# Scan levels in the projection, the first loads split over two queues, and q/k items ahead of gate and value items

## Chip, cores and metric

The kernel runs on one core of one Trainium2 chip, written in Bass: every engine has its own instruction stream, and streams wait for each other by semaphores. The metric is device time in microseconds. A profiled execution gives a span from its first to its last recorded instruction; the time that counts for it is a little longer.

## What is computed

Two layers of a backbone over 640 tokens: one tile of 128 context tokens and four tiles of latent tokens, width 1024, all in float32. A layer is

```python
h = rms_norm(x, norm1_g) * (1.0 + sc1) + sh1
qa, ia, fza, fzb, ga, qg, kg, vg, qw, kw, vw = split_proj(h @ w_in)      # 1024 -> 2560
o_a, s_a = hgrn_mixer(qa, ia, fza, fzb, ga, lb, a_norm_g, s_ctx)         # gated scans, both ways
o_g = blocked_attention(rope_2d(qg), ...)                                # all latent + cached keys
o_w = banded_attention(rope_2d(qw), rope_2d(kw), vw, ck_w, cv_w, sink)   # |t-s| <= 128
x = x + g1 * (jnp.concatenate([o_a, o_g, o_w], axis=-1) @ w_out)
h = rms_norm(x, norm2_g) * (1.0 + sc2) + sh2
x = x + g2 * moe(h, router_w, router_b, w_gate_up, w_down)               # top 2 of 16 experts
```

The shifts, scales and gates (sh1 to g2) are `silu(cond) @ mod_w + mod_b`, 6144 columns in twelve blocks of 512. A scan is `S = d * S + k v`, `o = q S`, for four heads, forward and backward, with a decay per channel.

## The kernel before

Each layer is a row of program sections (`nc.Block()`). At the end of a section all engines wait for each other. The sections that matter here:

**Setup** (lines 245 to 320): SyncE (SP) issues the loads of constants, masks and small vectors, then x (lines 267 to 269), four blocks of `mod_w` (line 271) and the layer's parameters (`load_params`, lines 240 to 243). SP's queue takes transfers in order, and an issue is held up while the queue is full.

**Norm 1** (lines 416 to 495): ScalarE squares x (line 465) and scales it (line 469). TensorE transposes it (lines 434 and 439), and in layer 0 it also computes the first four mod blocks (`cond_rows`, line 367; `turn_rows`, line 374). ScalarE and VectorE write the modulated `hT` (lines 476, 491, 494). SP loads `w_in` in five blocks; two of them wait until the transposes have read `xn`, which lies in their place.

**Projection** (lines 513 to 700): SP loads the cached keys and values (lines 516 to 519), TensorE transposes the keys (lines 533, 534), then come six items with turned output (four of gates, two of q and i, lines 544 and 545), five value items `ia` (line 571), ten q/k items `glob` and `win`, tile by tile (lines 577 and 580), and five `rest` items (line 574). An item is eight k-steps. Of a q/k item ScalarE copies the result (line 619), VectorE squares, sums and normalises it with a power from GpSimd (line 628) and rotates it (lines 691 to 696), TensorE transposes it (line 555), VectorE copies that into `qT` and `kT` (lines 652, 653).

**Attention** (lines 717 to 1240): 30 units (tile, head group, global or windowed); a loop of 32 steps does scores (line 911) of one unit, products with values (line 937) of the one before last, and transposes (line 923) of the last. VectorE finds the maxima (lines 1118, 1123), ScalarE takes the exponentials (line 1033), both copy turned probabilities (lines 1148, 1055), and VectorE writes the outputs of a pair of units (line 1159). Beside them run 81 **side steps**, three to a loop step, each waiting until the one before has been read (`s_free`):

- the scan's intra-tile scores by doubling: 8 levels x 5 tiles, four products each (level 0 on line 957, levels 1 to 7 on line 962, rows of 64). VectorE merges each result under a mask into `Am` (line 1173). After a level GpSimd multiplies keys and queries by the decays of the level's half blocks (lines 882, 887) and makes the next block products (line 874), and ScalarE merges the keys of both directions (line 1062). A level waits for both.
- after each level the next mod block: rows (line 367), ScalarE copy (line 1076), turn (line 374), VectorE add (line 1179).
- then ten pairs of keys (line 976) and state (line 980), and five outputs (lines 990, 995).

Behind the loop VectorE normalises the scan's output (lines 1230 to 1236), with a power from GpSimd (line 892), and the output projection follows (gate rows line 1249, `w_out` products line 1287). `sides_before` says which side steps a loop step has:

```python
            SIDE_START = 0
            THIRDS = 3
...
                return min(NSIDE, max(0, THIRDS * (step - SIDE_START) + part))
```

## Time and profile before

| | us |
|---|---|
| median of 3 runs | 1786.13 |
| lowest, highest | 1782.95, 1787.25 |
| the profiled execution | 1782.59 |
| its span | 1780.7 |
| TensorE busy in it | 1426.5 (80%) |
| VectorE, ScalarE, GpSimd busy | 567.3, 370.9, 198.7 |
| granted clock of TensorE, mean | 0.889 |

Stages of layer 0 by the stage table and the timeline: setup to 31.9, norm 1 to 63.8, projection from 79.2 to 260.8, attention to 501.8, output projection to 584, then norm 2, routing and experts; layer 1 begins its norm near 920. A busy TensorE is not one at its peak, and idle time of an engine that nobody waits for costs nothing.

### The profile page before, as it was taken

How to read it: one execution, taken by the hardware profiler on the slowest of the kernel's cores; microseconds unless marked ns; L12 is line 12 of the kernel's file. 1: busy time of each engine (PE TensorE's matmuls, PEld its weight loads, DVE VectorE, ACT ScalarE, POOL GpSimd, SP SyncE). 2: the span in 40 equal slices, each digit the busy share in tenths (PEclk: the TensorE clock that was granted, in tenths of full speed). 3: DMA queues.
4: the chain of work that ended last, by engine and by line, in shares of the span. 5: the costliest groups of instructions: out<-in, count | busy, mean ns of one | idle time of the engine just before them, and what ended most of it. 6: DMA issues, size and time to landing. Idle time of an engine off the chain costs nothing. (4 is left out here: it accounts for less than half of the span.)

```text
span 1780.7 us, 18938 instructions
## 1 busy us (share of the span) xinstructions
PE 1426.5 (80%) x6940; PEld 912.6 (51%) x6941; DVE 567.3 (32%) x1145; ACT 370.9 (21%) x745; POOL 198.7 (11%) x171
## 2 busy tenths in 40 slices
PE   0699998898879859999308999889886984999950
PEld 0357745677744724444105775557775454444420
DVE  0111524555421531111042053346443144111115
ACT  3111012334410301111031100233342021111113
POOL 0000113421010000000010010242201000000001
PEclk9799995999989869999758999789998995999985
DMA  9500014317010578999620000432200004799933
GB/s 330 189 1 3 1 42 153 121 70 275 1 47 0 209 271 290 369 369 352 233 84 7 0 4 3 145 134 105 98 1 0 0 30 165 255 368 365 359 114 142
DMA packets 111945, 254.12 MB, mean 143 GB/s; under 512 B 9832, under 2 KB 18432, under 8 KB 111872
## 3 DMA queue, kind: packets, MB, share of 16 engines
q1 hardware_dynamic: 93712, 199.64, 31.6%
q0 software_dynamic: 8064, 29.36, 4.5%
q10 hardware_dynamic: 10096, 24.12, 3.5%
q8 instruction: 49, 0.80, 0.2%
q14 instruction: 24, 0.20, 0.0%
HBM read 221.91 MB, written 34.34 MB: 144 GB/s over the span
## 5 line engine op out<-in xcount | busy, mean ns | idle before, releaser
L1670 PE MATMUL PS<-W,T 128*128 128x512 f32 x544 | 242.6, 599 | 4.5 <-ACT T L1712 4.5
L1670 PEld LDWEIGHTS PS<-W,T 128*128 128x128 f32 x544 | 104.3, 192 | 135.9 <-issue 130.1
L1287 PE MATMUL PS<-W,T 128*128 128x512 f32 x320 | 138.9, 593 | 2.3 <-ACT T L1300 2.3
L577 PE MATMUL PS<-W,hT 128*128 128x384 f32 x320 | 129.8, 487 | 0.0
L1688 PE MATMUL PS<-W,T 128*128 128x512 f32 x272 | 126.0, 607 | 1.4 <-ACT T L1736 1.4
L937 PE MATMUL PS<-T 128*128 128x64 f32 x864 | 112.1, 283 | 3.2 <-ACT T L1055 1.9
L937 PEld LDWEIGHTS PS<-T 128*128 128x128 f32 x864 | 105.1, 198 | 15.6 <-issue 8.5
L544 PE MATMUL PS<-hT,W 128*128 128x512 f32 x192 | 102.1, 615 | 0.0
L1287 PEld LDWEIGHTS PS<-W,T 128*128 128x128 f32 x320 | 60.2, 190 | 75.5 <-issue 72.7
L1761 DVE TENSOR_TENSOR T<-PS,T 128x256 f32<-128x256 f32 x34 | 14.5, 426 | 243.7 <-ACT T L1723 243.7
L911 PE MATMUL PS<-T 64*128 64x128 f32 (+3 forms) x480 | 70.0, 407 | 18.0 <-ACT T L1055 13.4
L580 PEld LDWEIGHTS PS<-W,hT 128*128 128x128 f32 x320 | 60.8, 190 | 42.3
L1628 POOL DMA_INDIRECT T<-h_rows,T x36 | 34.0, 946 | 428.8 <-PE PS L1660 323.2
L1757 DVE COPY T<-PS 128x1024 f32<-128x1024 f32 x34 | 41.7, 1226 | 119.4 <-PE PS L1688 119.4
L1173 DVE COPY_PREDICATED hT<-levelmask,PS 128x512 f32<-128x512 uint8 x80 | 59.1, 739 | 60.7 <-PE PS L962 47.1
L1723 ACT ACTIVATE T<-PS 128x256 f32<-128x256 f32 x34 | 13.1, 386 | 311.6 <-PE PS L1670 311.6
L962 PE MATMUL PS<-W 64*128 64x128 f32 x560 | 62.0, 348 | 19.6 <-ACT W L1062 10.7
L1688 PEld LDWEIGHTS PS<-W,T 128*128 128x128 f32 x272 | 50.1, 194 | 52.8 <-issue 52.8
L1033 ACT ACTIVATE T<-PS,small 128x640 f32<-128x640 f32 (+1 forms) x72 | 46.2, 647 | 119.7 <-DVE small L1137 94.7
L911 PEld LDWEIGHTS PS<-T 64*128 64x128 f32 x480 | 50.4, 207 | 39.4 <-DVE T L1148 21.4
L574 PE MATMUL PS<-W,hT 128*128 128x512 f32 x160 | 69.7, 592 | 0.0
L923 PE MATMUL PS<-cst,T 128*128 128x128 f32 x432 | 66.7, 301 | 0.0
(272 smaller groups left out, 1960.0 us busy)
## 6 DMA issues: line engine op xcount, KB each, us to landing
W<-in_w_gate_up SPq DMA_DIRECT2D x34, 2048.0 KB, 12.5
W<-in_mod_w SPq DMA_DIRECT2D x20, 2048.0 KB, 8.2
W<-in_w_down SPq DMA_DIRECT2D x34, 1024.0 KB, 10.6
y_rows<-T ACTq DMA_DIRECT2D x34, 512.0 KB, 8.8
W<-in_w_in SPq DMA_DIRECT2D x6, 2048.0 KB, 17.1
T<-in_mod_w SPq DMA_DIRECT2D x4, 2048.0 KB, 19.4
W<-in_w_out SPq DMA_DIRECT2D x2, 4096.0 KB, 13.8
y_rows<-cst SPq DMA_DIRECT2D x1, 7680.0 KB, 32.9
```

The costliest lines, as they stand in the source:

```text
L544: pe.matmul(PS[:, i % 2, :], lhsT, hT[:, k, P:TOK], start=(k == 0), stop=(k == KC - 1))
L574: last = pe.matmul(out, lhsT, wblk[:, B_REST, k, :], start=(k == 0), stop=(k == KC - 1))
L577: pe.matmul(out[:, 0:QW].rearrange("p (j v d) -> p j v d", v=KVH, j=G), lhsT, w[:, 0:QW].rearrange("p (v j d) -> p j v d", v=KVH, j=G), st ...
L580: last = pe.matmul(out[:, QW:512], lhsT, w[:, QW:512], start=False, stop=(k == KC - 1), skip_group_check=True)
L911: last = pe.matmul(PS[:, bank, at * P:(at + m) * P], qT[kv_rows, wnd, j, col(t)], kT[kv_rows, wnd, kt * P:(kt + m) * P], start=True, stop= ...
L923: last = pe.transpose(PS[:, bank, col(at)], pr[wnd][:, col(kv * len(keys) + n)], ident)
L937: last = pe.matmul(PS[:, 5, at:at + HD], src[:, col(kv * len(keys) + n)], v[:, kt, kv * HD:(kv + 1) * HD], start=(n == 0), stop=(n == len( ...
L962: last = pe.matmul(out, KM[rows_r, f, col(t)], both_ways(QD[rows_r].rearrange("p d f n -> p d (f n)"), at_t, P, h), start=True, stop=True)
L1173: dve.copy_predicated(Am[:, t, :, :], levelmask[:, lv:lv + 1, :].to_broadcast([P, AH, P]), PS[:, 6:8, 0:2 * P]).then_inc(s_free, 1)
L1287: last = pe.matmul(PS[:, 4 + 2 * (t % 2) + b, :], oT[:, t % 2, k, :], wout[:, k, col(b, 512)], start=(k == 0), stop=(k == KC - 1))
L1670: last = pe.matmul(PS[:, 2 + par, :], hgT[:, par, k, :], w[:, k, :], start=(k == 0), stop=(k == KC - 1))
L1688: last = pe.matmul(PS[:, 6 + b, :], haT[:, par, col(f)], w[:, f, col(b, 512)], start=(f == 0), stop=(f == 1))
```

## The change

- **Loads.** x is loaded from ScalarE's queue. The cache loads of layer 0 go into the setup, those of layer 1 into norm 1. Of the four first mod blocks two are issued in the setup, two in norm 1, with the q/i block of `w_in` behind them; the other four blocks of `w_in` are issued in the projection's section. The blocks' places in SBUF change, so that none waits for `xn`.
- **Order of the projection.** The q/i items and the value items come first, then the four gate items, then the q/k items of all tiles, then the rest (gate and value) items. The results go round three PSUM banks instead of four; transposes have one bank instead of two.
- **Levels.** The 8 levels x 5 tiles go out of attention into the k-loop of the last 15 items: a slot after every second k-step, five slots of products, then two without. They have two pairs of PSUM banks in turn. The level's products on GpSimd, the key merges on ScalarE and the masked copies on VectorE go with them. The work of VectorE on a q/k item is cut into four pieces, one per slot, and the squares of the norm go to ScalarE.
- **Attention.** 41 side steps are left, two to a loop step: keys, state, mod rows, mod turn, in turn. The scan's closing normalisation goes into the loop, one of its four parts in each of the steps 25 to 28.

```diff
+            sp.dma_start(ck[:, 0, :], cgk[0, l].rearrange("s h d -> s (h d)")).then_inc(s_cl, 16)
+            sp.dma_start(ck[:, 1, :], cwk[0, l].rearrange("s h d -> s (h d)")).then_inc(s_cl, 16)
+            sp.dma_start(vg[:, NT, :], cgv[0, l].rearrange("s h d -> s (h d)")).then_inc(s_cl, 16)
+            sp.dma_start(vw[:, NT, :], cwv[0, l].rearrange("s h d -> s (h d)")).then_inc(s_cl, 16)
...
-                sp.dma_start(x[:, 0, :], x_prompt[0]).then_inc(s_x[0], 16)
-                for t in range(1, NT):
-                    sp.dma_start(x[:, t, :], x_sample[0, (t - 1) * P:t * P, :]).then_inc(s_x[t], 16)
-                for n in range(MOD1):
-                    sp.dma_start(modw[:, n, :, :], mod_w[0, :, col(n, 512)].rearrange("(k p) n -> p k n", p=P))\
-                      .then_inc(s_mh[n], 16)
+                load_cache(sp, 0)
+                for n in range(2):
+                    load_first_mod(sp, n)
                 load_params(sp, 0)
...
             def _(act):
+                act.dma_start(x[:, 0, :], x_prompt[0]).then_inc(s_x[0], 16)
+                for t in range(1, NT):
+                    act.dma_start(x[:, t, :], x_sample[0, (t - 1) * P:t * P, :]).then_inc(s_x[t], 16)
...
                 def _(sp):
                     if layer == 0:
-                        for b in (B_GATES, B_QI, B_GLOB):
-                            load_win(sp, b, 0)
-                        sp.wait_ge(s_tr, 1 + KC)
-                        for b in (B_WIN, B_REST):
-                            load_win(sp, b, 0)
+                        for n in range(2, MOD1):
+                            load_first_mod(sp, n)
+                        load_win(sp, B_QI, 0)
+                    else:
+                        load_cache(sp, layer)
...
+            late = [(kind, t) for t in range(NT) for kind in ("glob", "win")] + [("rest", t) for t in range(NT)]
+            qk_late = [n for n, it in enumerate(late) if it[0] != "rest"]
+            NQ = len(qk_late)
+            REST0 = late.index(("rest", 0))
+            ITEM0 = NT
+            NLEV = len(LEVELS) + 1
+            SLOTS, FIRST_SLOT, GAP = 4, 3, 2
...
+            def level_in(q):
+                i = q - FIRST_SLOT
+                if i < 0 or i >= NLEV * (NT + GAP) or i % (NT + GAP) >= NT:
+                    return None
+                return i // (NT + GAP), i % (NT + GAP)
...
+            def merge_in(q):
+                i = q - FIRST_SLOT
+                if i < 0 or i % (NT + GAP) != NT + GAP - 1:
+                    return None
+                lv = i // (NT + GAP) + 1
+                return lv if lv < NLEV else None
...
+            def turn_after(n):
+                return qk_late.index(n - 2) if n - 2 in qk_late else None
...
+                    if layer == 0:
+                        for b in (B_GATES, B_GLOB, B_WIN, B_REST):
+                            load_win(sp, b, 0)
...
+                    def columns_turned(b, c0, parity):
                         for k in range(KC):
                             lhsT = wblk[:, b, k, col(c0)]
...
+                    pe.wait_ge(s_win[B_GATES], 16)
+                    for i in range(4):
...
                     def turn(m):
                         pe.wait_ge(s_rot, m + 1)
...
+                        for c in range(4):
+                            last = pe.transpose(PS[:, 3, col(c)], rr[:, m % 2, c, :], ident)
+                        last.then_inc(s_tp, 1)
+                    def level(lv, t):
+                        i = lv * NT + t
+                        if i == 0:
                             pe.wait_ge(s_cte, 1)
...
+                            pe.wait_ge(s_gr, 1)
+                            pe.wait_ge(s_qm, 2)
+                        if i >= 2:
+                            pe.wait_ge(s_lc, i - 1)
+                        if t == 0 and lv >= 1:
+                            pe.wait_ge(s_hm, lv)
+                            pe.wait_ge(s_km, lv)
+                        for a in range(AH):
+                            f, r = a // 2, a % 2
+                            rows_r = slice(64 * r, 64 * r + 64)
+                            out = PS[:, 4 + 2 * (i % 2) + r, col(f)]
+                            if lv == 0:
+                                for d in range(2):
+                                    last = pe.matmul(out, KK[rows_r, d, f, col(t)], QQ[rows_r, f, col(t)],
+                                                     start=(d == 0), stop=(d == 1))
+                                continue
+                            last = pe.matmul(out, KM[rows_r, f, col(t)],
+                                             both_ways(QD[rows_r].rearrange("p d f n -> p d (f n)"), f * TOK + t * P, P,
+                                                       LEVELS[lv - 1]), start=True, stop=True)
+                        last.then_inc(s_lp, 1)
...
+                    for n, (kind, t) in enumerate(late):
...
+                            if k == KC - 1:
+                                last.then_inc(s_z, 1)
+                            if k == 3 and turn_after(n) is not None:
+                                turn(turn_after(n))
+                            if k % 2:
+                                step = level_in(SLOTS * n + k // 2)
+                                if step is not None:
+                                    level(*step)
...
+                    pool.memset(Am, 0.0).then_inc(s_am0, 1)
+                    pool.wait_ge(s_gr, 1)
...
+                    for d in range(2):
+                        last = pool.tensor_tensor(qd[:, 1 - d, :], qq, fgate[:, d, :], ALU.mult)
+                    last.then_inc(s_hm, 1)
...
+                        flow(last)
+                    def update(lv):
+                        h = LEVELS[lv - 1]
+                        nb = 2 * TOK // (2 * h)
+                        product = fgate if h == 1 else BP[h]
+                        pool.wait_ge(s_lp, NT * (lv + 1))
+                        pool.wait_ge(s_hm, lv)
+                        for d in range(2):
+                            ks, qs = (0, 1) if d == 0 else (1, 0)
+                            of_q = pairs(product, d)[:, :, qs:qs + 1].to_broadcast([P, nb, h])
+                            last = pool.tensor_tensor(halves(kd, d, h, ks), halves(kd, d, h, ks), of_q, ALU.mult)
+                        last.then_inc(s_hk, 1)
+                        for d in range(2):
+                            ks, qs = (0, 1) if d == 0 else (1, 0)
+                            of_k = pairs(product, d)[:, :, ks:ks + 1].to_broadcast([P, nb, h])
+                            last = pool.tensor_tensor(halves(qd, 1 - d, h, qs), halves(qd, 1 - d, h, qs), of_k, ALU.mult)
+                        last.then_inc(s_hm, 1)
...
+                    block_products(fgate, BP[2])
+                    for q in range(SLOTS * len(late)):
+                        n = q // SLOTS - 1
+                        if q % SLOTS == 0 and n in qk_late and late[n][0] == "glob":
+                            pool.wait_ge(s_rd, late[n][1] + 1)
+                            pool.tensor_tensor(small[:, 88:96], small[:, 96:104], minus_half[:, 0:8],
+                                               ALU.pow).then_inc(s_rp, 1)
+                        step = level_in(q)
+                        if step is not None and step[0] >= 1 and step[1] == NT - 1:
+                            lv = step[0]
+                            update(lv)
+                            if lv < NLEV - 1:
+                                block_products(BP[2 * LEVELS[lv - 1]], BP[4 * LEVELS[lv - 1]])
...
+                    def level_copy(lv, t):
+                        i = lv * NT + t
+                        dve.wait_ge(s_lp, i + 1)
+                        if i == 0:
+                            dve.wait_ge(s_am0, 1)
+                        b = 4 + 2 * (i % 2)
+                        dve.copy_predicated(Am[:, t, :, :], levelmask[:, lv:lv + 1, :].to_broadcast([P, AH, P]),
+                                            PS[:, b:b + 2, 0:2 * P]).then_inc(s_lc, 1)
...
+                    def piece(m, s):
+                        t, w = m // 2, m % 2
+                        if s == 0:
+                            dve.wait_ge(s_ze, ITEM0 + qk_late[m] + 1)
+                        if w == 0:
+                            if s == 0:
+                                means(m)
+                            elif s == 1:
+                                normed(m)
+                            elif t > 0:
+                                rotated(m, s - 2)
+                            return
+                        if s == 0 and m >= 2:
+                            dve.wait_ge(s_tp, m - 1)
+                        if t == 0:
+                            if s == 0:
+                                dve.tensor_copy(rr[:, 1, :, :], zr[:, 1, :, :]).then_inc(s_rot, 1)
+                        elif s < 2:
+                            if t == 1 and s == 0:
+                                dve.wait_ge(s_co, 2 * 16)
+                            rotated(m, s)
+                    dve.wait_ge(s_par, 4 * 16 * (layer + 1))
+                    for n in range(len(late)):
+                        for s in range(SLOTS):
+                            if n - 1 in qk_late:
+                                piece(qk_late.index(n - 1), s)
+                            if s == 2 and turn_after(n) is not None:
+                                turned_evac(turn_after(n))
+                            step = level_in(SLOTS * n + s)
+                            if step is not None:
+                                level_copy(*step)
+                    for m in left_over:
...
-            for lv in range(NLEV):
-                side_steps += [("level", lv, t) for t in range(NT)]
-                side_steps += [("mod_rows", MOD1 + lv), ("mod_turn", MOD1 + lv)]
-            assert MOD1 + NLEV == 12
             for n in range(len(STATE_STEPS)):
                 side_steps += [("keys", n), ("state", n)]
+                if n < 12 - MOD1:
+                    side_steps += [("mod_rows", MOD1 + n), ("mod_turn", MOD1 + n)]
...
+            PER_STEP = 2
+            RMS_STEP = 25
...
-                return min(NSIDE, max(0, THIRDS * (step - SIDE_START) + part))
+                return min(NSIDE, max(0, PER_STEP * (step - SIDE_START) + min(part, PER_STEP)))
...
                     for step in range(U + 2):
+                        if RMS_STEP <= step < RMS_STEP + 4:
+                            scan_norm(step - RMS_STEP)
```

## Rows read from the trace of the kernel before

**Rows 1.** Stage table: stretch, length, busy PE, PEld, DVE, ACT, POOL, clock, DMA share, GB/s.
```profile
64.00:79.20 15.20, 0.00 (x0) 0.00 (x0) 0.00 (x0) 0.39 (x1) 0.00 (x0) 0.50 0.96 293
79.20:260.80 181.60, 180.55 (x714) 113.41 (x714) 48.19 (x115) 20.46 (x54) 8.19 (x6) 0.98 0.01 2
260.80:501.80 241.00, 197.49 (x1560) 158.32 (x1560) 123.38 (x270) 81.70 (x199) 59.90 (x47) 0.86 0.34 122
```
**Rows 2.** Timeline of the start: start, duration, engine, line, operation, wait.
```profile
7.87 16.39 SPq L271 DMA_DIRECT2D T<-in_mod_w  x4
...
24.30 5.29 SPq L240 DMA_DIRECT2D qkg<-in_q_norm_g  x1
...
31.97 1.06 ACT L465 ACTIVATE W<-x 128x1024 f32<-128x1024 f32 x1 [19.14 <-PEq L245]
...
63.09 0.72 DVE L494 TENSOR_SCALAR hT<-PS,scale,modc 128x128 f32<-128x128 f32 x2
...
71.98 2.42 SPq L516 DMA_DIRECT2D small<-in_cache_glob_k  x1
```
**Rows 3.** Stage table while the first loads run.
```profile
24.00:28.00 4.00, 0.00 (x0) 0.00 (x0) 0.00 (x0) 0.00 (x0) 0.00 (x0) 1.00 1.05 387
```
**Rows 4.** Timeline of TensorE, first instruction of layer 1's projection.
```profile
944.30 0.48 PE L533 MATMUL PS<-cst,small 128*128 128x128 f32 x1 [5.22 <-DMA T<-in_cache_win_v]
```
**Rows 5.** Timeline of TensorE in attention: a level unit and its follower.
```profile
343.32 0.72 PE L962 MATMUL PS<-W 64*128 64x128 f32 x8
343.96 2.44 PE L937 MATMUL PS<-T 128*128 128x64 f32 x20
```
**Rows 6.** Timeline of ScalarE in the projection: evacuation of a q/k item.
```profile
165.53 0.60 ACT L619 ACTIVATE T<-PS 128x512 f32<-128x512 f32 x1 [6.35 <-PE PS L580]
```
**Rows 7.** Attention's groups (busy, mean ns, idle before and why), then GpSimd's timeline.
```profile
L962 PE MATMUL PS<-W 64*128 64x128 f32 x280 | 31.2, 350 | 9.7 <-ACT W L1062 5.3 <-DVE hT L1173 2.5 <-POOL W L887 1.6
...
L1173 DVE COPY_PREDICATED hT<-levelmask,PS 128x512 f32<-128x512 uint8 x40 | 29.6, 739 | 30.1 <-PE PS L962 23.7 <-PE PS L957 6.3
...
L882 POOL TENSOR_TENSOR T<-T,hT 128x640 f32<-128x640 f32 x12 | 16.0, 1357 | 72.3 <-PE PS L962 72.3
...
L957 PE MATMUL PS<-T 64*128 64x128 f32 x80 | 9.4, 389 | 5.0 <-DVE hT L1173 5.0
...
293.53 3.62 POOL L882 TENSOR_TENSOR T<-T 128x640 f32<-128x640 f32 x2 [20.49 <-PE PS L962]
...
404.50 2.48 POOL L882 TENSOR_TENSOR T<-T,hT 128x640 f32<-128x640 f32 x2 [14.57 <-PE PS L962]
```
**Rows 8.** Timelines of GpSimd and VectorE in attention, then groups of the projection.
```profile
351.34 2.62 POOL L887 TENSOR_TENSOR W<-W,hT 128x640 f32<-128x640 f32 x2
351.44 1.25 DVE L1133 TENSOR_TENSOR small<-small,sink 128x2 f32<-128x2 f32 x1
...
L628 POOL TENSOR_TENSOR small<-small,minus_half 128x8 f32<-128x8 f32 x5 | 8.2, 1637 | 174.3 <-DVE small L669 174.3
...
L693 DVE TENSOR_TENSOR T<-T,cst 128x256 f32<-128x256 f32 x8 | 3.4, 425 | 0.3
```
**Rows 9.** Timeline of VectorE: outputs of pairs of units, and the stage's end.
```profile
431.21 0.42 DVE L1159 TENSOR_TENSOR W<-PS,small 128x256 f32<-128x256 f32 x1
...
445.25 0.42 DVE L1159 TENSOR_TENSOR W<-PS,small 128x256 f32<-128x256 f32 x1
...
462.18 0.43 DVE L1159 TENSOR_TENSOR W<-PS,small 128x256 f32<-128x256 f32 x1
...
473.82 0.42 DVE L1159 TENSOR_TENSOR W<-PS,small 128x256 f32<-128x256 f32 x1
...
483.69 0.42 DVE L1159 TENSOR_TENSOR W<-PS,small 128x256 f32<-128x256 f32 x1
...
492.88 0.42 DVE L1159 TENSOR_TENSOR W<-PS,small 128x256 f32<-128x256 f32 x1
...
499.79 1.49 DVE L1236 TENSOR_TENSOR W<-T,small 128x1280 f32<-128x1280 f32 x1 [1.97 <-POOL small L892]
```

463 lines of the change are left out of this document (204 added, 259 removed).

## Prediction

> **What bounds the kernel now.** I read the stage table first. The projection of layer 0 (79.2 to 260.8) has TensorE busy for 180.6 of 181.6 us: it is TensorE's own work, and whatever is put into it is paid for. The attention stage (260.8 to 501.8) has it busy for 197.5 of 241.0 us at a clock of 0.86 [rows 1]; layer 1 repeats both stages, and I count everything twice. So 43.5 us per layer of that stage are waits, and the change moves 40 small products from the stage with waits into the one without. Between 64.0 and 79.2 the engines do next to nothing [rows 1].
>
> Then the timeline of the start, to see what that silence is. SP hands out four blocks of mod_w (16.4 us for 4 issues, so it is held up by what is already queued), then the small parameter loads (5.3 us for the first), and only after them does its program section end; ScalarE takes up the norm at 31.97. The norm's last write ends at 63.8, the cache loads are issued at 72 because SP is still handing out w_in, and TensorE starts at 79.2 [rows 2]. In that stretch the DMA engines move 387 GB/s [rows 3]. In layer 1 the same cache loads cost TensorE 5.2 us of waiting [rows 4].
>
> **Start of layer 0.** The change takes two of the four mod_w blocks and the x loads out of SP's first section; x (2.6 MB) goes through ScalarE's queue, the cache loads go ahead of mod_w. Ahead of the parameters then stand about 1.2 MB of constants and masks, 0.3 of cache and 4.2 of mod_w, with x beside them. Before, the parameters got through when some 1.2 of the 4 blocks were still to come (issue ends 29.6; 12.3 MB in all would end near 36 at 387 GB/s) [rows 2, 3]. With the same rule and two blocks fewer (4.2 MB, 10.8 us) the section ends near 19; x used the slow first microseconds less than it could have, so I take 18 and as bounds 15 and 25. From ScalarE's first instruction to the last write of the norm it is 31.8 us [rows 2], which holds mod rows that need blocks 2 and 3; those land by about 36, before the 18 + 23 at which the last is used. Projection at 18 + 32.3 + 0.5 = 50.8, against 79.2: **28 us less** (21 to 31). The w_in block for q and i comes next in the queue, 2.1 MB or 5.4 us later (near 41), so it is there; the gate block is issued at 51 and is wanted only after 2 q/i items of 640 columns and 5 value items of 256. By 6.95 us for 8 steps of 512 columns [rows 6] these take 17.4 and 17.4 us, so near 85; the other blocks are wanted later still.
>
> **Start of layer 1.** Cache loads issued a section earlier: most of the 5.2 us go, not some 1.4 for the norm's last writes and the hand-over of sections: **3.8 us less** (3 to 4.5) [rows 4].
>
> **Projection: what is added.** Eight levels x 5 tiles = 40 units. A warm unit of levels 1 to 7 holds TensorE from 343.32 to 343.96, 0.64 us [rows 5]; one of level 0, with twice the products, twice that. 35 x 0.65 + 5 x 1.2 = 28.8 us. They now stand between the k-steps of the 512-column items, of which no row shows a price. The 0.64 was measured between foreign work too, so I add only 0.05 us a unit, 2 us in all (bounds 0 and 0.3 us a unit, 12 in all). Reordering the items adds and removes nothing: one of 512 columns goes on taking 6.95 us (6.35 of waiting and 0.60 of evacuation on ScalarE) [rows 6].
>
> Between two levels stand three slots of two k-steps, 5.13 us, or 5.6 where four transposes fall in them. In that time GpSimd must do its four products of the level: mean 1.36 us each, 1.81 at the first level and 1.24 at the last [rows 7], so about 7.3, 6.2, 5.5, 5.3, 5.1 and 5.0 us from the first to the sixth. Without anything in their way that leaves some 1.9 + 1.3 + 0.1 us of TensorE waiting, and 1.4 where a power for the norm (L628, 1.64 us [rows 8]) is ahead of them: 5 us.
>
> But something is in their way. VectorE's small operations end exactly where a GpSimd product ends: L1133, which touches 2 elements a row, took 1.25 us while L887 ran [rows 8]. The two exclude each other, one instruction at a time. In attention VectorE mostly reads PSUM; in the projection it has, per pair of items, three multiplications for the norm and twelve of 0.42 us for the rotation [rows 8], all from SBUF to SBUF. Followed instruction by instruction, with one VectorE operation let in after each product, level 2 goes so: the last product of level 1 ends 7.5 us into its item, GpSimd's four take 4 x 1.81 and three rotation operations of 0.42 come between, ready at 16.1; TensorE has three slots and four transposes (5.6) and stands there at 13.0: it waits 3.1 us. By the same steps level 3 waits 2.4, level 4 3.1 (the power stands ahead of the products), level 5 2.0 (the power stands behind them, so the norm and the copies of level 5 are late); levels 6 and 7 fall where no rotation is left, 0.1. Sum 10.7 us. VectorE's level copies (40 x 0.74 = 29.6 us [rows 7]) fit: 48.2 us of VectorE work become 78 in a stage of 220 [rows 1]. No step of the projection is moved past SP's stores.
>
> Sum: 28.8 + 2 + 10.7 = 41.5, **42 us more per layer** (34 to 54); the window becomes 181.5 + 42 = 223.5.
>
> **Attention: what goes.** In pairs of units (global and windowed of one head group) the time between outputs (L1159) is 9.87 us with no side work (473.82 to 483.69) and 14.04 with six side steps of keys and states (431.21 to 445.25) [rows 9]. New pairs have four: keys, state, mod rows, mod turn. They have less hand-over but the mod rows are longer, so I take the near row, 14.0 us, bounds 12.5 and 15.5, for pairs 3 to 7; 13.2 for pair 8 with four of keys and states (between the two); 16.9 for pair 9 with four output steps and 11.6 for pair 10 with one, as the pairs that end at 462.18 and 473.82; then 10.6 (one more key tile), 9.9, 9.9, 9.2, plus 1.5 for the closing norm, which now lies on VectorE between those units (four operations of 1.5 us, each covered by the scores of the next unit where VectorE has nothing to do). The first three pairs (context tile) cost more than their work: the very first state step now needs the state loads, which stand behind 4.2 MB of mod_w in the queue: 10.8 us at 387 GB/s [rows 3] and some 3 us around it, 14 us (before, nothing asked for them until the levels were done). VectorE waits for them with the next unit's maximum behind it, so TensorE stands too. Then 8.7 us a pair, of bare hand-overs: an estimate with no row of its own, it is 5.3 under the 14.0 of later tiles for the scores, transposes and weighing that the context tile hardly has (bounds 6 and 12). 14 + 3 x 8.7 = 40. Sum: 40 + 70 + 13.2 + 16.9 + 11.6 + 10.6 + 29 + 1.5 = 192.8, and of the tail (L1236 ended the stage at 501.3, 8 us behind the last output at 493.3 [rows 9]) 0.6 stays: 193.4, taken as 194, against 241: **47 us less per layer** (35 to 57). The check from the other side: the level products had 31.2 + 9.4 us of TensorE with 9.7 + 5.0 of waits ahead of them [rows 7], 55.3; with the tail 63; less the new 14 us wait, 49.
>
> **The sum.** 1782.6 (the profiled execution; its span is 1780.7) - 28 - 3.8 + 2 x (42 - 47) = 1740.8. The median of the runs shown is 1786.1, 3.5 more, so in medians 1786.1 - 41.8 = **1744**. The edit to the two stages nearly cancels; the loads are the gain.
>
> **Rivals.**
> 1. *GpSimd and VectorE do not collide* (the two stages overlap less often than I laid them, or attention loses more waits): projection +36, attention -50: 1786.1 - 31.8 - 28 = 1726. For it: the clash shows only on VectorE's side [rows 8], GpSimd's products were never seen to wait. Chance 0.14, for 1705 to 1728.
> 2. *Attention is paced by hand-overs, not by TensorE*: scores, maximum, exponential, copy in turn, with the side steps in line behind them. Then a step taken out gives nothing as long as others wait at the same place: pairs 3 to 7 stay at the 16.9 us of the slowest pair without levels [rows 9] instead of 14.0, 14.5 more, and the closing norm is uncovered at 6 us instead of 1.5. The stage is 213, the gain 28 for 47; 2 x 19 more: 1782. For it: 43.5 us of waits in the stage [rows 1], of which only 14.7 stand ahead of level products [rows 7]. Against: with no side work at all a pair falls to 9.87 [rows 9]. Chance 0.17, for 1766 to 1792: 0.10 faster, 0.06 no measurable change, 0.01 slower.
> 3. *Slower: VectorE wins the port.* In the rows GpSimd runs its products back to back and VectorE gets one in between. If a run of six rotation operations (2.5 us) goes ahead of each product instead, an update is 10 us longer minus the 1.8 already counted; at the four levels that meet rotations that is 32 us a layer, 64 in all: 1808. It decides from 21 us of extra waits a layer on. Against: L1133 was let in alone [rows 8]. Chance 0.07. The Trainium skill, SBUF — State Buffer, section "Who interferes with whom", calls this an exclusive lock held for a whole instruction and says that the order of issue decides who blocks; by it this rival's order is as allowed as mine, and a multiplication with both inputs in SBUF is among those that collide. The trace agrees on the whole instruction (1.25 us for 2 elements a row) and shows only one of the two orders.
>
> My forecast keeps 0.62, for 1728 to 1766. **Range**: 1715 to 1780, which leaves out the far end of rival 1, the upper part of rival 2 and rival 3, under 2 in 10. Runs of this kernel tell 0.3% (5.4 us) from no change. Faster by more: 0.62 + 0.14 + 0.10 = 0.86; within: 0.06; slower: 0.07 + 0.01 = 0.08.
>
> **What would show it.** TensorE's first projection product near 51 (right from 45 to 57); the wait for the cache gone in both layers. Projection windows of 223 us with TensorE waits in front of the level products, released by GpSimd, about 3 us at levels 2 to 4 and none at 6 and 7. VectorE multiplications of 1.3 us and more in place of 0.42 while products run. Attention windows of 194 us, 14 of them at the start behind the state loads, and no 8 us tail. It is wrong if attention stays over 205, if the projection passes 235, or if ScalarE still begins the norm after 25.

## The result, and the profile after

The changed kernel takes 1803.97 us (median of 4 runs, 1799.56 to 1806.74), the kernel before on the same chip 1784.54 (1782.29 to 1787.25). The ratio is 1.0088 with a 95% interval of 1.0052 to 1.0124: **0.9% slower**, where 1744 us and 2.3% faster were forecast. Another order of the same side steps then gave 1744.16 us, and the experiments say why. Of all executions behind the times of this document one, the fourth of run slot_early, was slow without a known reason (8134.28 us), and it is left out of that run's median.

The profiled execution of after is 1799.56 us long with a span of 1797.7, 17.0 longer than the span before. The stage table of after for layer 0, projection and attention (stretch, length, busy PE, PEld, DVE, ACT, POOL, granted clock, DMA share, GB/s):

```profile
53.20:277.20 224.00, 216.97 (x1074) 138.03 (x1073) 89.39 (x150) 32.94 (x66) 64.15 (x51) 0.99 0.12 39
277.20:495.10 217.90, 167.31 (x1201) 130.29 (x1201) 86.92 (x230) 71.24 (x192) 5.33 (x2) 0.85 0.37 134
```

Against [rows 1], the projection begins 26 us earlier, is 43 us longer and stands at a granted clock near full speed. The attention is only 23 us shorter: TensorE is busy 30 us less in it but waits 51 us for 44, at the same low mean clock. Its other products kept it busy for 163.2 us before (the trace's records without L957 and L962, merged), and the same ones do so for 167.3 now. The timelines of SP and ScalarE at the start of after answer [rows 2]:

```profile
7.70 2.78 SPq L241 DMA_DIRECT2D T<-in_mod_w  x2
10.52 6.84 SPq L254 DMA_DIRECT2D qkg<-in_q_norm_g  x1
...
20.38 0.38 SPq L241 DMA_DIRECT2D T<-in_mod_w  x1
20.40 1.06 ACT L478 ACTIVATE W<-x 128x1024 f32<-128x1024 f32 x1 [2.55 <-PEq L259]
```

The parameter loads are held up still (6.84 us for the first), yet they are through at 20 and ScalarE begins the norm at 20.40 instead of 31.97. At the start of layer 1, TensorE waits 1.35 us where [rows 4] had 5.22:

```profile
939.78 0.30 PE L576 MATMUL PS<-cst,small 128*128 128x128 f32 x1 [1.35 <-PEq L427]
```

TensorE's groups in the attention of after (line, busy, mean ns of one, idle before and what ended it):

```profile
L1061 PE MATMUL PS<-T 64*128 64x128 f32 (+2 forms) x240 | 37.6, 433 | 25.9 <-ACT T L1182 13.1 <-DVE T L1258 11.7 <-PEq L557 1.1
...
L380 PE MATMUL PS<-W,condT 128*32 128x512 f32 x128 | 21.9, 817 | 11.3 <-DVE T L1299 11.3
```

L1061 are the scores; TensorE waits 25.9 us ahead of them, for the copies of the transposed weights (L1182 on ScalarE, L1258 on VectorE). The same group in the kernel before waited 9.0:

```profile
L911 PE MATMUL PS<-T 64*128 64x128 f32 (+3 forms) x240 | 34.7, 404 | 9.0 <-ACT T L1055 6.7 <-DVE T L1148 1.1 <-PEq L513 1.1
```

One pair of steps of after shows the place (TensorE's timeline; L1073 transposes, L1061 scores, L1106 keys, L1087 weighing, L1110 state):

```profile
372.18 1.29 PE L1073 MATMUL PS<-cst,T 128*128 128x128 f32 x10
374.46 2.50 PE L1061 MATMUL PS<-T 64*128 64x384 f32 x8 [0.99 <-ACT T L1182]
376.89 0.69 PE L1106 MATMUL PS<-cst,T 128*128 128x128 f32 x2
377.37 2.58 PE L1087 MATMUL PS<-T 128*128 128x64 f32 x20
380.71 0.71 PE L1110 MATMUL PS<-T,W 128*128 128x128 f32 x4 [0.76 <-ACT W L1192]
381.26 0.82 PE L1073 MATMUL PS<-cst,T 128*128 128x128 f32 x6
383.08 1.15 PE L1061 MATMUL PS<-T 64*128 64x256 f32 x12 [1.00 <-DVE T L1258]
```

Between the transposes and the next scores stands nothing, and each time TensorE waits 1 us for the copy. Before, one side step of three stood there. (A plain product is two records of the timeline, a transpose is one: the x4 of L1110 are two products.)

**Where the time went**, from TensorE's first product of the projection, its first scores and the first product behind the attention, in us:

| stretch | before | after | difference |
|---|---|---|---|
| start to projection, layer 0 | 79.7 | 53.2 | -26.5 |
| projection, layer 0 / 1 | 181.1 / 180.4 | 224.1 / 224.1 | +43.0 / +43.7 |
| attention, layer 0 / 1 | 241.0 / 240.2 | 217.9 / 217.5 | -23.1 / -22.7 |
| behind it up to projection 1 | 443.0 | 444.9 | +1.9 |
| behind it to the end | 415.4 | 416.1 | +0.7 |

The sum is +17.0, as the spans say. The +1.9 hold the 3.9 us that layer 1's start gained and 5.8 lost behind layer 0's attention. Of the kernels below some are some 6 us shorter in that stretch and some are not, whatever was edited, and I give the 5.8 to no part of the change. The last stretch varies as well, from 413.9 to 424.6 us, in kernels that differ only ahead of it. So a part is judged by its stage's length, and the kernel's time alone does not settle less than some 10 us.

### The profile page after: what moved, and what is told of

It reads as the page before. It is cut to its first block and busy times, and to the rows that moved or that the text cites. A ratio compares the mean times of both kernels' runs of the same rounds, so it can differ in the third digit from the quotient of the medians.

```text
span 1797.7 us, 18955 instructions
## 1 busy us (share of the span) xinstructions
PE 1448.3 (81%) x6940; PEld 912.0 (51%) x6941; DVE 577.4 (32%) x1135; ACT 375.0 (21%) x755; POOL 201.5 (11%) x171
## 3 DMA queue, kind: packets, MB, share of 16 engines
q1 hardware_dynamic: 92992, 197.01, 30.8%
## 5 line engine op out<-in xcount | busy, mean ns | idle before, releaser
L657 PE MATMUL PS<-W,hT 128*128 128x384 f32 x320 | 137.5, 512 | 0.0
L1087 PEld LDWEIGHTS PS<-T 128*128 128x128 f32 x864 | 105.0, 198 | 25.5 <-issue 19.5
L1061 PE MATMUL PS<-T 64*128 64x128 f32 (+2 forms) x480 | 74.2, 429 | 50.8 <-ACT T L1182 26.1
L1087 PE MATMUL PS<-T 128*128 128x64 f32 x864 | 111.1, 282 | 3.2 <-ACT T L1182 1.9
L582 PE MATMUL PS<-hT,W 128*128 128x512 f32 x192 | 98.3, 594 | 0.0
L825 DVE COPY_PREDICATED W<-levelmask,PS 128x512 f32<-128x512 uint8 x80 | 58.2, 727 | 109.6 <-PE PS L637 87.4
L1873 DVE TENSOR_TENSOR T<-PS,T 128x256 f32<-128x256 f32 x34 | 14.5, 426 | 243.6 <-ACT T L1835 243.6
L1061 PEld LDWEIGHTS PS<-T 64*128 64x128 f32 x480 | 52.0, 216 | 74.5 <-DVE T L1258 62.6
L380 PE MATMUL PS<-W,condT 128*32 128x512 f32 x336 | 61.5, 873 | 26.5 <-DVE T L1299 21.5
L655 PE MATMUL PS<-W,hT 128*128 128x512 f32 x160 | 76.2, 610 | 0.0
L637 PE MATMUL PS<-W 64*128 64x128 f32 x560 | 52.8, 308 | 12.0 <-issue 9.8
## 6 DMA issues: line engine op xcount, KB each, us to landing
W<-in_w_gate_up SPq DMA_DIRECT2D x34, 2048.0 KB, 12.4
W<-in_w_down SPq DMA_DIRECT2D x34, 1024.0 KB, 10.6
W<-in_w_in SPq DMA_DIRECT2D x6, 2048.0 KB, 17.4
```

Of the source, the lines that this page charges most:

```text
L380: last = pe.matmul(PS[strip, bank, :], condT[:, k, :], w[:, k, :], start=(k < 4), stop=(k >= 4), skip_group_check=True)
L582: pe.matmul(PS[:, parity, :], lhsT, hT[:, k, P:TOK], start=(k == 0), stop=(k == KC - 1))
L637: last = pe.matmul(out, KM[rows_r, f, col(t)], both_ways(QD[rows_r].rearrange("p d f n -> p d (f n)"), f * TOK + t * P, P, LEVELS[lv - 1]) ...
L655: last = pe.matmul(out, lhsT, w, start=(k == 0), stop=(k == KC - 1))
L657: pe.matmul(out[:, 0:QW].rearrange("p (j v d) -> p j v d", v=KVH, j=G), lhsT, w[:, 0:QW].rearrange("p (v j d) -> p j v d", v=KVH, j=G), st ...
L825: dve.copy_predicated(Am[:, t, :, :], levelmask[:, lv:lv + 1, :].to_broadcast([P, AH, P]), PS[:, b:b + 2, 0:2 * P]).then_inc(s_lc, 1)
```

## The experiments

Two theories stood at first. By my prediction's sum, a level step costs TensorE's time wherever it stands, and the attention of after must have got something new that eats the gain. By the **cover theory**, the level steps of the old attention stood in time in which TensorE would have waited anyway, so the attention gives little back for them while the projection pays in full. The runs will show a third thing, the granted clock, beside both.

Each ratio is to the kernel before on the same chip; the chips of the runs differ. A median is of 3 to 10 executions, "one time" is a single one. Stage lengths are measured as in the table above, in one profiled execution, layer 0 / layer 1.

| run | us (median) | ratio, 95% interval | projection | attention |
|---|---|---|---|---|
| loads | 1753.56 | 0.9814, 0.9792 to 0.9837 | 180.1 / 178.6 | 240.1 / 239.6 |
| loads_norm | 1745.12 | 0.9767, 0.9746 to 0.9787 | 178.6 / 178.6 | 238.5 / 232.1 |
| early_mods | 1796.18 | 1.0047, 1.0016 to 1.0078 | 225.5 / 224.1 | 213.5 / 209.8 |
| att_empty | 1778.46 | one time | 179.8 / 180.6 | 236.7 / 237.1 |
| filler | 1826.09 | 1.0218, 1.0164 to 1.0273 | 225.6 / 224.1 | 227.0 / 230.0 |
| three | 1778.94 | 0.9946, 0.9913 to 0.9980 | 225.5 / 224.1 | 203.0 / 196.3 |
| proj_empty | 1753.78 | one time | 201.3 / 199.9 | 217.5 / 217.9 |
| proj_nopool | 1778.79 | one time | 216.2 / 216.2 | 218.0 / 220.0 |
| pairs | 1803.53 | 1.0079, 1.0039 to 1.0119 | 228.0 / 225.8 | 218.7 / 219.3 |
| all3 | 1773.85 | 0.9899, 0.9867 to 0.9930 | 228.4 / 225.8 | 194.5 / 194.4 |
| att_double | 1832.65 | one time | 181.3 / 180.5 | 265.4 / 257.6 |
| att_nopool | 1781.49 | one time | 181.3 / 180.5 | 232.2 / 227.8 |
| slot | 1744.16 | 0.9774, 0.9732 to 0.9817 | 225.6 / 224.1 | 190.6 / 188.3 |
| att_refill | 1793.59 | 1.0038, 1.0017 to 1.0058 | 181.3 / 180.6 | 245.0 / 238.0 |
| att_empty2 | 1781.19 | 0.9967, 0.9949 to 0.9986 | 181.2 / 180.6 | 234.4 / 237.1 |
| slot_early | 1731.45 | 0.9706, 0.9678 to 0.9735 | 222.4 / 224.1 | 181.1 / 179.0 |

### The loads alone, and the loads with the closing norm

Run loads is the kernel before with the change's first loads; its main lines:

```diff
-                for t in range(1, NT):
-                    sp.dma_start(x[:, t, :], x_sample[0, (t - 1) * P:t * P, :]).then_inc(s_x[t], 16)
-                for n in range(MOD1):
-                    sp.dma_start(modw[:, n, :, :], ...
+                load_cache(sp, 0)
+                for n in range(2):
+                    load_first_mod(sp, n)
```

> The kernel before with one part of the change alone: the first loads split (x through ScalarE's queue, two mod_w blocks ahead of the parameters and two behind, the cache loads of each layer one section earlier). The order of the projection and of the attention is that of before. If the parts add up as the trace of after says, the projection of layer 0 starts at 52 to 54 (before 79.2), the one of layer 1 some 4 us nearer to its norm, the rest is untouched: 1784.5 - 26.3 - 4.2 = 1754 us. Rival: the early start only helps because the q/i block comes first in the new order, and here the gates block of before arrives too late: then less than 15 us of the 26 are left, 1765 us or more.

Measured: 1753.56 us, and the projection of layer 0 starts at 55.5. The gain of the loads is what it should be, and it needs no new order of the projection's items. By difference the rest of the change costs some 49 us (1.0088 against 0.9814).

Run loads_norm adds the change's scan_norm, called in the loop (steps 27 to 30, where the change has 25 to 28) instead of behind it:

```diff
+                        if RMS_STEP <= step < RMS_STEP + 4:
+                            scan_norm(step - RMS_STEP)
```

> The kernel before with the new first loads and with the closing norm of the recurrence spread over steps 27 to 30 of the attention loop instead of behind it. The level steps stay in the attention. In the kernel before, the last output stands at 492.9 and the stage ends at 501.8; with the norm inside the loop, the stage should end near 494 to 496: 6 to 8 us less per layer, so 1754 - 14 = 1740 us, faster than before by 2.5%. If the norm's four operations of 1.5 us are not covered by the scores of the next units, half of it is left: 1747 us.

Measured: 1745.12 us, 8.4 less than loads for 14 expected. Layer 1 gained 7.5 us of its attention and layer 0 only 1.6.

### What the level work costs the projection

proj_empty and proj_nopool cut the change's level steps. In both, GpSimd's updates touch one block:

```diff
-                            of_q = pairs(product, d)[:, :, qs:qs + 1].to_broadcast([P, nb, h])
+                            of_q = pairs(product, d)[:, 0:1, qs:qs + 1].to_broadcast([P, 1, h])
```

proj_empty has, besides, one product of 2 columns per step:

```diff
-                        for a in range(AH):
+                        for a in range(1):
...
-                            out = PS[:, 4 + 2 * (i % 2) + r, col(f)]
+                            out = PS[:, 4 + 2 * (i % 2) + r, 0:2]
```

> The changed kernel with the level steps of the projection emptied in place: one product of 2 columns instead of four or eight of 128, masked copies of 2 columns, GpSimd's updates on the first block only (the recurrence's result is not computed; block products, merging of keys and the place of every step are kept). What the level work costs the projection is what goes: by my sum 28.8 of products + 2 for their insertion + 10.7 of waits = 41.5 us per layer; by the trace of after 36.7 of TensorE's time + 6 of waits. Either way the stage goes from 224 to 182 to 185 us and the kernel to about 1722 us. The rival here is that the emptied steps still cost 0.2 to 0.3 us each because they break into the stream of products: then 190 us or more, 1735 us.

> The changed kernel with GpSimd's updates in the projection cut to the first block of each level (the recurrence's result is wrong by that), while TensorE does all level products. If the price of a level step (0.90 us in the stream) is the products' own, only TensorE's waits ahead of the levels go, 6 us per layer: stage at 218, kernel at 1792 us. VectorE's multiplications of the rotation, 1.2 to 2.1 us while GpSimd works, should take 0.42 us again. If my term of 10.7 us for the collision was right and the products cost 0.72 us, the stage should lose 10 us or more: 1783 us.

The emptied projection is 201.3 us, not 182: the rival of that expectation holds, and its 0.2 to 0.3 us a step is still too little. TensorE's timeline of proj_empty:

```profile
146.50 0.38 PE L659 MATMUL PS<-W,hT 128*128 128x128 f32 x2
146.81 0.38 PE L637 MATMUL PS<-W 64*128 64x2 f32 x2
147.12 0.91 PE L656 MATMUL PS<-W,hT 128*128 128x384 f32 x2
...
149.05 0.38 PE L637 MATMUL PS<-W 64*128 64x2 f32 x2
```

From emptied step to emptied step it is 2.24 us, with two k-steps of 0.87 between them: a single product of 2 columns costs 0.50 us of the stream. In after, a full one of four products costs 2.61 - 1.74 = 0.87. The wait of 2.13 us ahead of the first row is one of four such; the others are 1.49, 1.31 and 1.06 us:

```profile
169.40 1.03 PE L637 MATMUL PS<-W 64*128 64x128 f32 x8 [2.13 <-issue]
...
173.61 0.75 PE L637 MATMUL PS<-W 64*128 64x128 f32 x8
...
176.22 0.75 PE L637 MATMUL PS<-W 64*128 64x128 f32 x8
```

Without GpSimd's updates the stage is 216.2, 7.9 us less, and TensorE is busy without a gap; 216.2 is 35.1 over the projection of before. The products cost more than these 35.1: the projection of before starts at a granted clock of 0.50 (79.2 to 84.0) and that of after at 1.00 (53.0 to 58.0), and the largest group of the first items takes 49.1 us (L582 in after) for 51.4 (L544 in before, the same 96 records). So of the 43 us some 37.5 are products, 8 are what the updates cost, and some 2.5 came back by the clock at the start.

The 8 are not all collision. TensorE's four waits sum to 6.0 us, where the prediction had 5 without a collision and 10.7 with it. VectorE's side of the collision is plain, in after (GpSimd, then VectorE):

```profile
165.29 4.01 POOL L778 TENSOR_TENSOR W<-W,T 128x640 f32<-128x640 f32 x2
165.53 2.10 DVE L860 TENSOR_TENSOR T<-T,cst 128x256 f32<-128x256 f32 x1
167.56 2.03 DVE L861 TENSOR_TENSOR T<-T,cst 128x256 f32<-128x256 f32 x1
```

The same VectorE line in proj_nopool:

```profile
163.89 0.42 DVE L860 TENSOR_TENSOR T<-T,cst 128x256 f32<-128x256 f32 x1
```

GpSimd's side is small: its four products of this level take 3.80 + 4.01 = 7.81 us (161.52 to 169.30) where the same four in the attention of before took 3.62 + 3.67 = 7.29 (293.53 to 300.78).

Run pairs does two level steps after every fourth k-step instead of one after every second:

```diff
-                            if k % 2:
-                                step = level_in(SLOTS * n + k // 2)
-                                if step is not None:
-                                    level(*step)
+                            if k % 4 == 3:
+                                for q in (SLOTS * n + k // 2 - 1, SLOTS * n + k // 2):
+                                    step = level_in(q)
+                                    if step is not None:
+                                        level(*step)
```

> The changed kernel with the level steps of the projection done two at a time: instead of one after every second k-step, two after every fourth. Products, copies and updates are the same, in the same order. In the run with emptied level steps a step of one 2-column product still cost 0.50 us of the stream (the next two k-steps started 2.24 us later instead of 1.74). If that is the price of leaving the stream of 128-row products and coming back, it is paid 20 times less per layer: 20 x 0.5 = 10 us, 1804 - 20 = 1784 us. If it is the product's own price (weights of 128 columns), nothing changes: 1804 us.

Measured: nothing gained. In the timeline of pairs, TensorE's two steps together stand from the last k-step to the next one so:

```profile
150.04 0.38 PE L660 MATMUL PS<-W,hT 128*128 128x128 f32 x2
150.35 1.59 PE L637 MATMUL PS<-W 64*128 64x128 f32 x16
151.87 0.91 PE L657 MATMUL PS<-W,hT 128*128 128x384 f32 x2
```

1.83 us from k-step to k-step instead of the bare 0.22, and the k-step behind is 0.10 longer: 1.71 for eight products, 2 x 0.87 done singly. My theory of a price for leaving the stream is wrong. Products in the stream cost 0.21 to 0.22 each when there are four or eight and 0.50 when there is one of them; what makes up the 0.50 was not tried.

### What the level work cost the attention

Four kernels edit the attention of before. att_empty empties products, masked copies and updates; att_nopool the updates alone; att_double does each product twice:

```diff
-                            for a in range(AH):
+                            for a in 2 * list(range(AH)):
```

att_refill is att_empty with four useless products of 128 rows into each emptied step (eight at level 0), att_empty2 is att_empty once more:

```diff
+                            for a in range(AH if lv else 2 * AH):
+                                pe.matmul(PS[:, 7, col(a % 4)], va[:, 1, col(a % 2)], va[:, 2, col(a % 2)],
+                                          start=True, stop=True)
```

> The kernel before, with the level steps of the attention emptied in place: each of the 40 does one product of 2 columns instead of four (eight) of 128, the masked copy takes 2 columns, and GpSimd's updates run on the first block only (so the recurrence's result is not computed; the block products and the merging of keys on ScalarE are kept, and so is the place of every other step). My prediction's sum says that the level work costs the attention about 40 us per layer (31 us of products, 10 us of waits ahead of them): the stage goes from 241 to about 201, the kernel to 1704. The cover theory (most products stood in time in which TensorE would have waited for scores, maximum, exponential and copy anyway) says 15 to 25 us per layer: the stage at 216 to 226, the kernel at 1735 to 1755.

> The kernel before with GpSimd's updates in the attention cut to the first block of each level (the recurrence's result is wrong by that), and all level products done. It tells what the collision of GpSimd and VectorE costs the attention. By my prediction some 10 us of waits ahead of the products go, of which 1.6 are put down to GpSimd; GpSimd is busy 59.9 us of the stage. If VectorE's maxima and copies are held up by it, 5 to 10 us less per layer, 1765 to 1775 us; if the attention covers that too, less than 2 us, 1781 to 1785 us.

> The kernel before with every product of the level steps in the attention done twice, into the same place. The level groups took 31.2 + 9.4 = 40.6 us per layer. Bound by TensorE's work, the attention goes from 241 to 281 us and the kernel to 1866 us. If two thirds of added work is taken in by waits and by a higher granted clock, as with the useless products added to the changed kernel (28 us of work, 9 to 12 us longer), the attention goes to 251 to 258 us, 1805 to 1820 us, and the granted clock of the first 160 us (0.66, 0.80, 0.95, 0.91 in 40 us each before) rises.

Emptied, the attention is 3 to 4 us shorter, less than either theory said. Emptying the updates alone takes 8.8 and 12.4 us off. So taking the products (and VectorE's masked copies) away on top of that made the stage **longer**, by 4.5 and 9.3 us in single executions on two chips, by 2.2 and 9.3 with att_empty2 below. The stage tables show what did it. att_empty:

```profile
300.00:340.00 40.00, 35.57 (x183) 26.17 (x182) 11.74 (x39) 13.08 (x29) 2.17 (x9) 0.59 0.30 105
...
380.00:420.00 40.00, 37.08 (x225) 30.41 (x223) 14.07 (x38) 12.14 (x27) 1.05 (x4) 0.70 0.35 129
```

att_nopool, where TensorE has the products still:

```profile
300.00:340.00 40.00, 33.54 (x286) 24.15 (x288) 19.71 (x50) 15.28 (x39) 4.14 (x14) 0.93 0.46 158
...
380.00:420.00 40.00, 35.77 (x291) 29.16 (x290) 18.61 (x41) 14.90 (x33) 2.21 (x10) 0.91 0.39 145
```

The granted clock is 0.59 and 0.70 instead of 0.93 and 0.91 (0.80 and 0.91 in before), a mean over stretches at full speed and at half of it. In att_empty TensorE is as busy as before, 197.5 us in the stage, with fewer and slower instructions, and its waits did not rise, as the cover theory needs, but fell from 43.5 to 39.2 us. Its groups (busy, mean ns of one, idle before):

```profile
L937 PE MATMUL PS<-T 128*128 128x64 f32 x432 | 61.4, 301 | 1.6 <-ACT T L1052 0.9 <-DVE T L1145 0.7
L911 PE MATMUL PS<-T 64*128 64x128 f32 (+2 forms) x240 | 40.7, 459 | 11.1 <-ACT T L1052 7.8 <-DVE T L1145 2.2 <-PEq L513 1.1
L923 PE MATMUL PS<-cst,T 128*128 128x128 f32 x216 | 37.0, 324 | 0.0
L367 PE MATMUL PS<-W,condT 128*32 128x512 f32 x128 | 25.6, 941 | 1.1 <-DVE hT L1170 1.1
```

And the same ones of the kernel before, beside L911 above:

```profile
L937 PE MATMUL PS<-T 128*128 128x64 f32 x432 | 56.1, 283 | 1.6 <-ACT T L1055 0.9 <-DVE T L1148 0.7
...
L923 PE MATMUL PS<-cst,T 128*128 128x128 f32 x216 | 33.9, 304 | 0.0
...
L367 PE MATMUL PS<-W,condT 128*32 128x512 f32 x128 | 19.3, 731 | 4.4 <-DVE hT L1173 4.4
```

Identical work took 5.3 + 6.0 + 3.1 + 6.3 = 20.7 us longer. The emptied level groups gave back about as much: 40.6 us of products [rows 7] became 20.3.

> The kernel before with emptied level steps and emptied GpSimd updates, and into each emptied step useless products of TensorE: 4 of 128 rows by 128 columns (8 at level 0) into a bank that nobody reads, 0.71 us for four, some 32 us per layer (the recurrence's result is not computed). If the emptied kernel lost to a low granted clock what it saved in work (same groups of instructions 24.8 us longer than in the kernel before, at 0.59 and 0.70 in two windows of 40 us), the useless work brings the clock back and the stage is no longer, or shorter: 228 to 237 us, kernel at 1762 to 1778 us, clock of the stage 0.88 or more. If the lower clock was chance and TensorE's work counts, 32 us per layer on top: 1835 us.

> The same kernel as att_empty once more (level steps and updates of the attention emptied), beside att_refill on one chip. If the low clock belongs to this order of work: stage at 237 us, clock of 300 to 340 us below 0.7, kernel near 1778 us. If it was chance, the stage should come out at 215 to 225 us in at least one of the layers, 1755 us or less.

The low clock is no chance: att_empty2 has it again (0.63 and 0.74 in the two stretches, 1781.19 us in the median of 9). The useless work of att_refill brings the clock of these stretches to 0.93 and 0.91, but does not make the kernel faster, against its expectation: against att_empty2 it costs 10.6 us in layer 0 and 0.9 in layer 1, 12.4 us in the medians.

The useless work is more than the 32 us that the expectation gives it. The row that it took for four products, in before, is x4, which is two:

```profile
424.49 0.71 PE L980 MATMUL PS<-T,W 128*128 128x128 f32 x4 [1.21 <-ACT W L1079]
```

Four of these useless products (x8) take 0.99 us of the stream in att_refill, from 348.36 to 349.35, where the granted clock is 1.00. That makes some 45 us per layer, an estimate from this one row. The whole group in layer 0, part of it at the lower clock and overlapping its neighbours, is busy 56.2 us:

```profile
L952 PE MATMUL PS<-T 128*128 128x128 f32 x360 | 56.2, 308 | 6.3 <-ACT W L1062 4.6 <-DVE hT L1173 1.6
```

Against att_empty2 the products that both have keep TensorE busy for 155.8 us of that stage instead of 180.6, as the clock of the stage is 0.93 for 0.79, and it waits 28.8 us instead of 39.5. That is how 10.6 us remain of the added work.

att_double says what work costs where neither helps. Its level groups grew from 40.6 us to 51.4 + 13.4 = 64.8, so the second half of a group costs less than the first:

```profile
L962 PE MATMUL PS<-W 64*128 64x128 f32 x560 | 51.4, 332 | 10.6 <-ACT W L1062 5.4 <-POOL W L887 2.7 <-DVE hT L1173 2.5
L957 PE MATMUL PS<-T 64*128 64x128 f32 x160 | 13.4, 326 | 3.9 <-DVE hT L1173 3.9
```

The added 24.2 us made the stage 24.4 us longer, at the same mean clock (0.86) and with nearly the same waits (42.6 us for 43.5); in layer 1 TensorE was busy 17.9 us more and the stage 17.4 longer. So work added beside the level products was paid in full, in the one execution there is, and no wait covered it. Taking the products away saved nothing because the clock fell and the rest took longer: the cover theory has the outcome, and not the reason.

The Trainium skill (TensorE: Matmul & The Clock Gate, section HAM oscillation — how this bites in real kernels) describes a kernel whose clock falls again and again because TensorE waits for transfers between short groups of products. Here the waits are for other engines, and their sum is smaller in att_empty than in before; which waits lowered the clock no run shows.

### The pace of the changed attention

Run filler puts useless products behind the transposes of the first 20 steps of after:

```diff
+                                for a in range(AH):
+                                    pe.matmul(PS[:, 7, col(a)], KK[:, 0, a // 2, col(1 + a % 2)], va[:, 1, col(a // 2)],
+                                              start=True, stop=True)
```

> The changed kernel with useless products added to its attention: after the transposes of each of the first 20 steps, TensorE does 8 products of 128 rows by 128 columns into the bank that the level products used before; nobody reads them. At 0.71 us for four of this form (such a group in the trace of before, 424.5) that is 28 us of TensorE's time per layer. My prediction's sum took the attention to be bound by TensorE's work: then it is 28 us longer per layer, 1804 + 57 = 1860 us. Cover theory: they lie where TensorE would wait for the copy of the transposed weights, and they keep the granted clock up in the first 60 us, which was 0.54 in the changed kernel; so at most 5 us per layer, 1796 to 1812 us, with the granted clock of the stage higher than in the changed kernel (0.85).

Measured: 9.1 and 12.5 us longer, more than the cover theory's 5. The added work is not 28 us here either: a step's eight products (x16) take 1.88 us at a granted clock of 1.00 (353.14 to 355.02), and 20 steps have them, 37.6 us. The products that both kernels have keep TensorE busy for 153.4 us instead of 167.3, and it waits 34.5 us instead of 50.6: in this place added work is covered in part, as it is not in att_double. The clock of 300 to 340 rises from 0.54 (after) to 0.89. Filler:

```profile
300.00:340.00 40.00, 33.87 (x258) 26.41 (x254) 11.01 (x38) 9.38 (x35) 0.00 (x0) 0.89 0.45 158
```

Run three does three side steps per step:

```diff
-            PER_STEP = 2
+            PER_STEP = 3
```

Run early_mods loads the first mod_w block of the attention at the end of the projection and the states ahead of the second, and puts mod steps ahead of keys and states. SP's part:

```diff
+                    sp.dma_start(modw2[:, 0, :, :], mod_w[layer, :, col(MOD1, 512)].rearrange("(k p) n -> p k n", p=P))\
+                      .then_inc(s_mw[0], 16)
...
-                    load_mod2(MOD1)
-                    load_mod2(MOD1 + 1)
                     sp.wait_ge(s_hg, 1)
...
-                    for n in range(MOD1 + 2, 12):
+                    for n in range(MOD1 + 1, 12):
                         load_mod2(n)
```

all3 is early_mods, three and pairs in one.

> The changed kernel with three side steps of the attention per step instead of two, so that one stands again between the transposes of a unit and the scores of the next, and the side steps end at step 14 instead of 21. The work is the same. If TensorE's work sets the pace, nothing changes: 1804 us. If the hand-overs do, the wait of 1.0 us ahead of the scores (between 374 and 399 us in the changed kernel) falls to the 0.3 to 0.55 us of the kernel before at 14 steps, and the copies of the mod rows and keys overlap more: 4 to 8 us less per layer, 1788 to 1796 us.

> The changed kernel with the attention's first loads in another order: the first mod_w block of the attention is issued at the end of the projection, the state loads ahead of the second, and the mod steps ahead of the keys and state steps of the same number. It takes the wait of TensorE for the state loads away (11.3 us at 294.1 in layer 0 of the changed kernel) and puts nothing in its place if the pace behind it is kept: 1804 - 2 x 11 = 1782 us. If the wait only moves to the mod_w loads (the first three pairs are bound by transfers), less than 5 us per layer: 1795 us or more.

> The changed kernel with three edits of the runs before together: three side steps per step of the attention, the mod_w and state loads of the attention in the other order, and the level steps of the projection in twos. If they add up, 1804 - 25 - 8 - 20 = 1751 us; if the wait for the state loads is already covered by three side steps and the pairs bring nothing, 1780 us. In neither case should it beat the kernel before with its new loads and the closing norm in the loop (1745 us), as the level steps cost the projection more than they cost the attention.

three gained 15 and 21 us per layer, where 4 to 8 were forecast. all3 did not add up to its 1751 us: its attention is 194 us, but pairs brought nothing and its projection is 2 to 4 us longer. early_mods gained 4 to 8 us per layer; TensorE waits for the second mod_w block instead of the states, and the clock is higher first (0.70 in 300 to 340, 0.54 in after) and lower in the next two stretches of 40 us (0.83 and 0.91 against 0.91 and 1.00 in after):

```profile
294.88 3.64 PE L380 MATMUL PS<-W,condT 128*32 128x512 f32 x16 [5.26 <-DMA W<-in_mod_w]
```

three left it open whether the crowding or the place did it. Run slot keeps two per step and moves the second behind the transposes, on all engines:

```diff
-                return min(NSIDE, max(0, PER_STEP * (step - SIDE_START) + min(part, PER_STEP)))
+                return min(NSIDE, max(0, PER_STEP * (step - SIDE_START) + (0, 1, 1, 2)[part]))
```

> The changed kernel with the same two side steps per step, but the second one after the transposes instead of behind the weighing (places 0 and 2 instead of 0 and 1, on all engines). Nothing else changes; the side steps end at step 20 as before. If what the change lost is the cover between a unit's transposes and the next scores (TensorE waits 25.9 us ahead of scores in the attention of the changed kernel, 9.1 in that of before), these waits fall to about 12 us and the stage from 218 to 204 to 208 us: 1776 to 1784 us. If three per step helped because the work is crowded into fewer steps, or by the clock of the first 60 us, this run stays at 214 us or more, 1797 us or more.

Measured: **1744.16 us**, attention 190.6 and 188.3, well under the 204 to 208 of the expectation. No instruction was added or taken away. The same pair of steps as above, in slot:

```profile
374.83 2.34 PE L1087 MATMUL PS<-T 128*128 128x64 f32 x20
377.01 1.04 PE L1073 MATMUL PS<-cst,T 128*128 128x128 f32 x8
378.38 0.71 PE L1110 MATMUL PS<-T,W 128*128 128x128 f32 x4 [0.33 <-ACT W L1192]
379.02 1.15 PE L1061 MATMUL PS<-T 64*128 64x256 f32 x12
380.15 1.92 PE L380 MATMUL PS<-W,condT 128*32 128x512 f32 x16
```

The state products (L1110) stand where TensorE waited for the copies, and the scores follow without a wait. The groups of slot:

```profile
L1061 PE MATMUL PS<-T 64*128 64x128 f32 (+2 forms) x240 | 34.2, 400 | 12.6 <-ACT T L1182 8.1 <-DVE T L1258 3.2 <-PEq L557 1.1
```

Waits ahead of scores fall from 25.9 to 12.6, which is 13.3 of the 27.3 us. Most of the other half is the clock: TensorE is busy 154.7 us for 167.3 with the same products (L1061 3.4 us less, L387 2.3, L1087 2.1), and the stage tables say why, 0.54 and 0.91 in the stretches 300 to 340 and 340 to 380 of after against 0.78 and 1.00 here. Slot:

```profile
300.00:340.00 40.00, 34.40 (x222) 21.82 (x215) 14.95 (x50) 12.62 (x44) 0.00 (x0) 0.78 0.59 208
340.00:380.00 40.00, 36.97 (x316) 29.23 (x314) 20.66 (x61) 16.62 (x43) 0.00 (x0) 1.00 0.32 109
```

The place is the only thing that was edited; how much of the 27.3 us is cover and how much the clock that followed, no run separates further.

With the pace mended, the order of loads was tried again:

> The changed kernel with the second side step behind the transposes (run slot, 1744 us, attention 190.6 and 188.3 us) and with the attention's mod_w and state loads in the other order (run early_mods). If the wait for the state loads (11.2 us ahead of L380 in layer 0 of slot) is paid in full, the attention falls to 178 to 181 us and the kernel to 1722 to 1726 us. If it is covered by the transfers behind it, as in early_mods (where the first mod_w block was waited for 5.3 us instead, and the stage fell by 4 to 8 us), 1730 to 1737 us.

Measured: 1731.45 us, 2.9% faster than before and better than both kernels; the attention is 9.5 and 9.3 us shorter than in slot, as the first branch of the expectation says. The wait for the states (11.25 us at 297.75 in slot) is paid nearly in full here, and a wait of 6.02 us for a mod_w block remains. The kernel gained 12.7 us and not 18.8: the stretch behind layer 1's attention, which was not edited, is 423.4 us long here and 413.9 in slot.

## Why the prediction failed, step by step

**Start of layer 0: right.** ScalarE at 20.40 (18 forecast), the first product at 53 (50.8), 26.5 us less (28, bounds 21 to 31). **Start of layer 1: right**, the wait went from 5.22 to 1.35, 3.9 us (3.8).

**Projection: right in sum, by errors that cancel.** 43.0 and 43.7 us more for 42. The products cost more: I took the 0.65 that a level unit has in the attention and added 2 us in all for the insertion, where a unit in the stream takes 0.87 and one of level 0 twice that, some 37.5 us instead of 30.8. Some 2.5 us were saved by the clock at the start, which was not in the sum. The waits cost less: 2.13 + 1.49 + 1.31 + 1.06 = 6.0 us at TensorE, 7.9 by proj_nopool, for 10.7. They stand at the four levels that were named. VectorE's multiplications of 2.0 to 2.1 us beside GpSimd's products are the collision as described, but it hardly delayed GpSimd (7.81 us for 7.29 at the first level), and 6.0 is nearer to the 5 us reckoned without it.

**Attention: wrong, 23 us for 47.** Of the some 24 us that are missing in layer 0, pairs 3 to 8 (the hand-overs) make 14.5, the first six steps 6.4 and the last pair 7.3; pairs 9 and 10 gave 3.6 back. The step that failed is "I take the near row, 14.0 us" for pairs 3 to 7, with the words ahead of it that four side steps for six leave less hand-over. The row came from a pair whose side steps stand in all three places of a step [rows 9], and two of them covered the copy between transposes and scores. The change's `min(part, PER_STEP)` leaves that place empty, and I read the count in the diff and not the place. Pairs 3 to 7 took 16.2 us on average in after and 12.4 in slot. This is the mechanism of the second rival, hand-overs that pace the stage. It forecast 213 for the stage and 1782 us, got 0.17, and was worked out for the wrong reason (that the emptied places would stay expensive, and that the closing norm would not be covered; the four pairs with it took 41.1 us, as the main forecast had them). The other part is the clock, for which the sum has no term: TensorE's products took 167.3 us of the stage in after and take 154.7 in slot, where the granted clock is 0.91 for 0.85. Three other terms of the stage were off:

- The last pair of steps, 30 and 31, was left out of the sum. It is 7.3 us. In slot it is made up for by the pairs at 12.4 us, and so slot's 190.6 and 188.3 come near to the 194 forecast. That slot's 1744.16 us is the forecast's number is luck of that kind, and no sign that the sum was right.
- The wait for the state loads was taken at 14 and was 11.3 us, but the context pairs at 8.7 were too cheap for a granted clock of 0.54: the first six steps took 46.4 us for 40. In slot they took 41.3.
- Pair 9 took 14.2 us for 16.9 and pair 10 took 10.7 for 11.6, and pair 8 took 16.9 for 13.2.

**The check from the other side misled.** It counted 55.3 us of products and waits of the level steps as what the stage would give back [rows 7]. The runs show that this time cannot be taken back at its price: emptying 20.3 us of the products made the others 20.7 us longer, although added products were paid in full there (24.2 us of them cost 24.4). The clock of the kernel before [rows 1] was read as a property of the stage, while it moved with the work in it: 0.78 emptied, 0.86 in before, 0.93 refilled.

**Rival 3 is out**: the waits are 6 to 8 us per layer, and it needed 32. **Rival 1** is out as a whole: VectorE's multiplications do take 2.0 us for 0.42 beside GpSimd's products, the projection grew by 43 us where it had 36, and the attention gained 23 where it had 50. Its term for the waits, 5 us, was better than mine. What the collision by itself costs no run shows, as proj_nopool and att_nopool take the updates away and the collision with them.

## What to carry over

A side step in a software pipeline is worth what it covers: before the number of steps per round is changed, list which hand-over each place covers, and keep the one between an engine's last product and the copy that the next product waits for. Take the price of an inserted group from a row with the same neighbours, and count what a row's xN are before a price is taken from it. Do not count the time of small products as a gain in a stage where the granted clock is under full: here their removal lowered it further. A change of several parts is best timed in parts; here one part was worth 33 us, the other cost 49, and another place for one side step in it gave 60 back.

## What the runs showed of the hardware

- Taking 20.3 us of small TensorE products out of a stage with waits made the remaining ones 20.7 us longer, at a granted clock of 0.59 instead of 0.80 in one stretch of 40 us; useless products in their place (some 45 us) brought 0.93, and the stage was still 10.6 and 0.9 us longer. Doubling the products instead (24.2 us more of them) left the clock at 0.86 and cost 24.4 us. The same level group takes 0.72 us where the granted clock is 1.00 (343.2 to 344.1) [rows 5] and 1.23 where it is 0.50 (285.6 to 287.2), in the first 40 us of the old attention:

```profile
285.84 1.23 PE L962 MATMUL PS<-W 64*128 64x128 f32 x8 [0.20 <-DVE hT L1173]
```

- One product of 64 rows and 2 columns between products of 128 rows costs the stream 0.50 us, four of 128 columns 0.87, eight 1.71.
- Two-input multiplications of VectorE in SBUF of 0.42 us took 2.03 to 2.10 us beside a GpSimd product, in turns with it, while GpSimd's four products of that level took 7.81 us (7.29 in the attention of before). The Trainium skill (SBUF — State Buffer, section Who interferes with whom) calls it an exclusive lock for a whole instruction, and the rows agree: each VectorE operation ends about 2.0 us after the one ahead of it, as long as one of GpSimd's two products.
